# w_down by seven Strassen products, each accumulated over all pairs of feature tiles, placed behind the gate and up products

## The reference

```
x = x + rmsnorm(mix, post_mix_norm[l])
h = rmsnorm(x, pre_ffn_norm[l])
f = (jax.nn.silu(h @ ffn_w_gate[l]) * (h @ ffn_w_up[l])) @ ffn_w_down[l]
x = x + rmsnorm(f, post_ffn_norm[l])
# second layer
x32 = x.astype(jnp.float32)
y = x32 * lax.rsqrt(jnp.mean(x32 * x32, axis=-1, keepdims=True) + EPS)
z = jnp.einsum('bsd,de->bse', h, w_in)
```

## Time and profile before

| what | value |
|---|---|
| time, median of 3 runs | 2336.81 us (2334.63 to 2337.70) |
| time of the profiled execution | 2337.01 us |
| its span | 2335.1 us |
| mean granted TensorE clock | 0.973 of full speed |
| PE busy | 2153.8 us, 92% of the span, 10931 matmul instructions |
| PEld busy | 1812.1 us, 78% |
| DVE busy | 1183.2 us, 51%, 1698 instructions |
| ACT busy | 793.0 us, 34%, 1442 instructions |
| POOL busy | 906.1 us, 39%, 611 instructions |
| DMA | 125.95 MB, mean 54 GB/s |

### The profile page before, as it was taken

The page is one execution under the profiler, slowest core; times in us unless marked ns, Lnnn a source line. Parts: engine busy times, 40 slices in busy tenths (PEclk is TensorE's granted clock), DMA queues, the critical chain, the costliest instruction groups (busy, mean ns, idle before and its releaser), DMA issues. The chain is left out here.

```text
span 2335.1 us, 29185 instructions
## 1 busy us (share of the span) xinstructions
PE 2153.8 (92%) x10931; PEld 1812.1 (78%) x10931; DVE 1183.2 (51%) x1698; ACT 793.0 (34%) x1442; POOL 906.1 (39%) x611
## 2 busy tenths in 40 slices
PE   6999988688997899999999996888999999999997
PEld 5788877578775788888888875777887888888886
DVE  4443505867436735555555557678996154201132
ACT  4333225455224342222222224237775122000112
POOL 1222321332236766666666665230000332323334
PEclk9999999889999999999999997999999999999999
DMA  4121311020212111111111132210000111111131
GB/s 153 37 50 42 82 53 24 14 52 32 99 46 82 47 53 54 46 46 46 54 55 55 55 118 77 96 37 1 1 1 24 45 46 45 48 52 45 54 118 72
DMA packets 164187, 125.95 MB, mean 54 GB/s; under 512 B 25316, under 2 KB 144848, under 8 KB 163920
## 3 DMA queue, kind: packets, MB, share of 16 engines
q1 hardware_dynamic: 148576, 91.77, 13.5%
q10 hardware_dynamic: 15472, 32.31, 3.8%
HBM read 106.77 MB, written 17.30 MB: 53 GB/s over the span
## 5 line engine op out<-in xcount | busy, mean ns | idle before, releaser
L940 POOL TENSOR_SCALAR w_hi<-w_raw 128x1024 fp32r<-128x1024 f32 x113 | 130.6, 1155 | 990.2 <-issue 919.5
L1059 PE MATMUL gemm<-h_hi,w_hi 128*128 128x512 f32 x1072 | 424.3, 396 | 8.4 <-POOL h_lo L969 4.6
L1060 PE MATMUL gemm<-h_lo,w_hi 128*128 128x512 f32 x1072 | 419.6, 391 | 0.0
L1061 PE MATMUL gemm<-h_hi,w_lo 128*128 128x512 f32 x1072 | 419.5, 391 | 0.0
L943 POOL TENSOR_TENSOR w_lo<-w_raw,w_hi 128x1024 fp32r<-128x1024 f32 x113 | 283.0, 2504 | 9.4
L1059 PEld LDWEIGHTS gemm<-h_hi,w_hi 128*128 128x128 f32 x1072 | 203.0, 189 | 53.3 <-issue 8.1
L1061 PEld LDWEIGHTS gemm<-h_hi,w_lo 128*128 128x128 f32 x1072 | 202.6, 189 | 43.0
L1060 PEld LDWEIGHTS gemm<-h_lo,w_hi 128*128 128x128 f32 x1072 | 202.9, 189 | 40.6
L1873 DVE TENSOR_TENSOR acc<-acc,gemm 128x1024 f32<-128x1024 f32 x80 | 97.7, 1221 | 116.1 <-PE gemm L1080 115.9
L936 POOL TENSOR_TENSOR w_lo<-wsum,w_hi 128x512 fp32r<-128x512 f32 x100 | 136.8, 1368 | 28.4 <-ACT w_hi L1507 22.1
L1507 ACT ACTIVATE w_hi<-wsum 128x512 fp32r<-128x512 f32 x100 | 63.3, 633 | 200.3 <-POOL wsum L923 197.3
(11 more groups left out here) (413 smaller groups left out, 4404.7 us busy)
## 6 DMA issues: line engine op xcount, KB each, us to landing
w_raw<-in_w_in SPq DMA_DIRECT2D x60, 512.0 KB, 3.8
w_raw<-in_ffn_w_gate SPq DMA_DIRECT2D x22, 512.0 KB, 3.8
w_raw<-in_ffn_w_up SPq DMA_DIRECT2D x22, 512.0 KB, 4.1
w_raw<-in_ffn_w_down SPq DMA_DIRECT2D x22, 512.0 KB, 4.0
w_raw<-in_w_out SPq DMA_DIRECT2D x16, 512.0 KB, 3.7
x_spill<-x ACTq DMA_DIRECT2D x4, 2048.0 KB, 6.6
xin<-in_x SPq DMA_DIRECT2D x8, 512.0 KB, 6.4
x<-in_x ACTq DMA_DIRECT2D x1, 4096.0 KB, 15.9
```

The lines of the kernel that those rows point to most:

```text
L940: gp.tensor_scalar(hi[:], raw[key % 4][:], 1.0, 0.0, ALU.mult, ALU.add).then_inc(pool_hi, 1)
L1059: mm(o, hi[:, k, m], act[0][:, k, t], start=k == 0, stop=False)
L1060: mm(o, hi[:, k, m], act[1][:, k, t], start=False, stop=False)
L1061: last = mm(o, lo[:, k, m], act[0][:, k, t], start=False, stop=k == kt - 1)
```

## The change

w_down is no longer applied pair by pair within the gate and up loop. Now all the gate and up products come first (`f` of every pair is kept: most of it in SBUF, 16 blocks of 128x512 are written to DRAM and read back), and behind them stands a stage of seven products M4, M7, M1, M5, M3, M2, M6, each accumulated in four banks over 11 pairs: 77 items `("dm", (i, x))` of 12 matmuls. The two-by-two blocks are: of f, the feature tile of the pair (m) by the half of the tokens (t); of w_down, the same feature tile by the half of the columns. Product i reads one f block or a sum or difference of two, and one weight block or a sum or difference of two. Even products use the side banks, odd ones the gemm banks (`SIDE`). After each product its four banks are copied (ACT) or added or subtracted (DVE) into `acc`, at items `("de", (i, c))` four blocks into the next product.

For each block n the work is: DVE adds or subtracts two f blocks (`fsum`, L2196 of the kernel after; in M7, M1, M5, M2 and M6, since M4 and M3 read a single block) and two weight blocks (`wsum`, L853; in M4, M7, M1, M3 and M6); ACT rounds both to `ring_0` (L1706) and `w_hi` (L1679); DVE subtracts to get `ring_1` (L2205) and `w_lo` (L862). The ring and the weight slots each hold four blocks. At item x DVE does the sums of block x+5 and the low parts of block x+4. SP loads the one or two weight blocks of 256 KB of each item by a DMA each, and at blocks 5 and 12 of the list eight 256 KB blocks of f each from DRAM. POOL has only the gain multiplications in this stage (item `dsq`), and the last of these is on DVE. The post norm, the residual and the next norm of the first half of the tokens are within M2 and M6 (items `rows`, `res`, `nsq`, `nk`); those of the second half come after the first halves of the two q2 units.

The core of the diff:

```diff
+DOWN = (
+    ("M4", [(1, 1)], None, SUB, [(1, 0), (0, 0)], [(0, 0, None), (1, 0, None)]),
+    ("M7", [(1, 0), (1, 1)], SUB, ADD, [(1, 0), (1, 1)], [(0, 0, ADD)]),
+    ("M1", [(0, 0), (1, 1)], ADD, ADD, [(0, 0), (1, 1)], [(0, 0, ADD), (1, 1, None)]),
+    ("M5", [(0, 0), (1, 0)], ADD, None, [(1, 1)], [(0, 1, None), (0, 0, SUB)]),
+    ("M3", [(0, 0)], None, SUB, [(0, 1), (1, 1)], [(0, 1, ADD), (1, 1, ADD)]),
+    ("M2", [(0, 1), (1, 1)], ADD, None, [(0, 0)], [(1, 0, ADD), (1, 1, SUB)]),
+    ("M6", [(0, 1), (0, 0)], SUB, ADD, [(0, 0), (0, 1)], [(1, 1, ADD)]),
+)
+SIDE = (0, 2, 4, 6)
+CLOSING = (6,)
+PAIRS = tuple(range(9)) + (10, 9)
+ND = len(PAIRS)
...
-        if p + 1 < NF // 2:
-            run([("down", (p - 1, h, x)) for h in range(2) for x in range(4)])
         s += [("mul", (by["up", 2 * p], i)) for i in range(7)]
-    s.append(("load", 8))
-    run([("down", (NF // 2 - 2, h, x)) for h in range(2) for x in range(4)])
-    s.append(("load", 9))
-    run([("down", (NF // 2 - 1, h, x)) for h in range(2) for x in range(2)])
-    s.append(("rows", (1, 0)))
-    run([("down", (NF // 2 - 1, 0, x)) for x in range(2, 4)])
-    s += [("resid", (1, 0)), ("nsq", (2, 0))]
-    run([("down", (NF // 2 - 1, 1, x)) for x in range(2, 4)])
-    s.append(("rows", (1, 1)))
-    begin([("q2", 4), ("q2", 0)], [("norm", (2, 0)), ("load", 1), ("nsq", (2, 1))],
-          [("norm", (2, 1)), ("load", 2)])
+    between = {(4, 2): [("load", 8)], (4, 6): [("dsq", (0, 0))], (5, 3): [("dsq", (0, 1))], (5, 4): [("rows", (1, 0))],
+               (5, 5): [("res", 0)], (5, 6): [("res", 1)], (5, 7): [("res", 2)], (5, 8): [("res", 3)], (5, 9): [("nsq", (2, 0))], (6, 2): [("load", 9)], (6, 4): [("load", 1)],
+               (6, 6): [("dsq", (1, 0))]}
+    for i in range(7):
+        for x in range(ND):
+            s += [("dm", (i, x))] + [("de", (i - 1, x))] * (0 <= i - 1 not in CLOSING and x < 4) + between.get((i, x), [])
+            s += [("nk", x - 2)] * (i == 6 and 2 <= x <= 9)
+        if i in CLOSING:
+            s += [("de", (i, c)) for c in range(4)] + [("dsq", (1, 1)), ("dt", i)]
+    begin([("q2", 4), ("q2", 0)],
+          [],
+          [("rows", (1, 1)), ("resid", (1, 1)), ("nsq", (2, 1)), ("norm", (2, 1)), ("load", 2)])
...
# SP
+                if w in (down0 + 5, down0 + 12):
+                    part = int(w == down0 + 12)
+                    if part == 0:
+                        sp.wait_ge(f_out, 16 * len(spilled))
+                    gemm_product(sp, (last_up, 6 if part else 4))
+                    for key, n in sorted(spilled.items(), key=lambda x: x[1]):
+                        if n // 8 == part:
+                            sp.dma_start(f_at[key][:], f_dram[n]).then_inc(f_in[part], 16)
...
# PE
+            def down(i, x):
+                at_end = i in CLOSING and x >= ND - 2
+                if at_end and x == ND - 2:
+                    return
+                blocks = (ND - 2, ND - 1) if at_end else (x,)
+                for y in blocks:
+                    pe.wait_ge(w_split, job_of["dm", i, y] + 1)
+                    pe.wait_ge(N["d_low"], ND * i + y + 1)
+                for c in range(4):
...
+                        mm(o, f[0][:, hslice(c)], hi, start=y == 0, stop=False)
+                        mm(o, f[0][:, hslice(c)], lo, start=False, stop=False)
+                        last = mm(o, f[1][:, hslice(c)], hi, start=False, stop=y == ND - 1)
...
# DVE
+                elif kind == "dm" and (j[0] not in CLOSING or j[1] < ND - 2):
+                    n = ND * j[0] + j[1]
+                    block_sum(n + 5)
+                    weight_sums(it)
+                    block_low(n + 4)
+                    weight_lows(it)
...
# POOL
+                elif kind == "dsq" and j != (1, 1):
+                    t, h = j
+                    pool.wait_ge(gain_loaded, 32)
+                    for pair in range(2):
+                        pool.wait_ge(N["sq_part"], 16 + 8 * t + 4 * h + 2 * pair + 2)
+                        x = acc[:, 4 * t + 2 * pair:4 * t + 2 * pair + 2, 512 * h:512 * h + 512]
+                        step(gp.tensor_tensor(x, x, over(gbc2[:, 512 * h:512 * h + 512], 2), ALU.mult), "acc_gained")
```

## The result

The changed kernel takes 2318.4 us (median of 4 runs, 2317.6 to 2320.3) where the kernel before took 2336.5 on the same chip: a ratio of 0.9924, 95% interval 0.9907 to 0.9942. I had said 2310 with a range of 2295 to 2338. Every median here is of runs that agree with one another; one of the four runs of the kernel with the read-backs spread took 7460.6 us, which nothing on record explains, and is left out of its median. The profiled executions differ by 16.6 us (spans 2335.1 and 2318.5).

What follows compares the result with a forecast made beforehand. PE bounds the old loop, DVE the new stage from M7 on. DVE's queue of 236.7 us plus 5.4, 15.6 and 3 gives 260.7 against 287.5 before: 26.8 saved, 2310 us, range 2295 to 2338.

Steps and rivals of the forecast that it cites:

- my signs of being wrong: Down stage and loop: DVE idle in M7 while PE waits, `wsum` waiting for `w_raw`, clock clearly under 1, gate/up gaps.
- item 5 (low part of block 9): Start of the down stage: DVE, held by loads, is through at about 20.5 us, and PE isn't held up.
- items 39 to 49: Down stage, second of two stretches of eleven blocks with three DVE instructions each, plus additions: 26.7 us of DVE's queue.
- The wait behind the second 2 MB: Within items 6 to 27: DVE waits about 3.6 us for block 12's weights behind the second read-back of f.
- slower, by the loads: Rival for the down stage: w_down loads and f share SP's queue, blocks take longer, 2352 us; chance 0.06.
- The lock: Items 50 to 60: POOL's gain multiplications hold up DVE instructions with two SBUF inputs, four times 2.4, 9.6 us.
- my tail: From the last down matmul to the second norm half: additions, squares, gain, residuals and norm, 15.6 us.
- The cold clock: After the stage: PE idle for nearly 5 us, then at a lower clock for a while, costing 3 us.
- What I had at nothing: Gate and up loop without down products: keeps its length, no gaps in the products.
- The PE-bound stage at 2287: Rival: the lock costs little and reads stay hidden, so PE bounds the stage; 2287 us, half 2298; together chance 0.16.
- Hand-overs: Rival: crossings between DVE, ACT and PE expose 0.3 us on each of 71 items, 2331 us; chance 0.20.
- The clock: Rival: PE's waits in M2 to M6 lower its clock, blocks take 5.4 us, 2350 us; chance 0.08.

Runs made afterwards that it cites:

- The control without Strassen: Changed kernel's order, read-backs one by one, with eight ordinary block products (1056 matmuls, not 924) and no sums of f or weights: 2314.8 us.

## Why the prediction was right, and where its sum was off

**The order of things held.** DVE is the bound from M7 on; PE's waits are on DVE's `w_lo`; POOL's gain multiplications make single DVE instructions last 2.3 to 2.8 us; the down stage has 924 matmuls. The experiments carry this: 39.9 us added to DVE cost 32.9. One of my signs of being wrong came all the same: waits of `wsum` for `w_raw`, 11.5 us.

**Term by term**, where DVE finishes its last step of a block (us from the start of the stage, predicted and then measured): item 5 (low part of block 9) 20.5 and 26.4; items 6 to 27 69.9 and 70.6; M5's stretch 26.7 and 26.9; the next, items 39 to 49, 26.7 and 31.5; items 50 to 60 with the first residual 43.3 and 42.5; items 61 to 71 with the last `h_lo` 48.2 and 48.5; item 72 1.4 and 3.5. The sum is 236.7 against 249.8. Then 5.4 and 6.8 us to the last matmul, and 15.6 and 18.8 us to the second norm half: 257.7 against 275.4.

**The step that was mis-sized is the loads.** "They can start when the fourth-last product is done, so block 5's weights land at about 7 to 8 us" forgot that SP's queue is in order. The read-backs stand behind block 4's loads, which wait for DVE's first `w_lo`; they go out 2.0 us after the start of the stage, block 5's loads at 6.7, and `wsum` of block 5 starts at 13.35. From there DVE did the five blocks up to item 5 without a wait, in 13.0 us as my sum had it, so all of the 5.9 us (26.4 in place of 20.5) lies in that landing. PE, which I had as not held up there, waited 3.9 us in the first 16. "Items 39 to 49: 26.7" had no load at all in it, though item (4,2) in the same table of the change issues 2 MB on the other queue: 4.8 us. Spreading both gave back 9.9 of these 10.7 in the median, 8.6 in the traces. The wait behind the second 2 MB, 3.6 us in my sum, was right (3.77). I had put a price on transfers as a rival ("slower, by the loads", 2352) and not in the sum where they belonged, at a tenth of that size.

**The lock.** 9.6 us predicted for `dsq` inside items 50 to 60, at 2.4 us for each of four instructions. The three gain multiplications of two instructions each cost DVE 9.9 in all, but not all there: four lengthened instructions are inside (7.8 us), one is the last item's `w_lo` (the 2.1 us of item 72), and POOL's low part of the next weights, which my tail didn't have, hits the gain multiplications on DVE. That pair took 4.89 us where two undisturbed ones take 2.45: 2.4 of the 3.2 us by which the tail is longer.

**The cold clock** came to the size that I gave it, for a longer wait than I had: in 1437 to 1446 us PE is idle for 7.9 us, not nearly 5, and the windows of PE after it (columns as in the earlier trace rows) are

```profile
1446.00:1460.00 14.00, 14.00 (x87) 13.11 (x86) 6.01 (x8) 5.50 (x8) 0.00 (x0) 0.85 0.23 90
```

where the same work before was at 1.00. From the start of the second norm half to the end the kernel takes 873.0 us, before 869.9: 3.1 for the 3 us predicted. The same happens inside the stage, behind the 8.0 us wait: 0.67 in 1395 to 1401 us, part of it at the 1.2 GHz level. There it is free: where the transposes come one item later, the clock is at 1.00 in 1392 to 1410 us and the time is the same (2318.3).

**What I had at nothing** came out as a gain: the gate and up loop, without its down products, takes 382.7 us from 787.45 to 1170.11, where it took 389.9 before with the down products' 195.9 taken off. The 7.2 us can be placed: before, PE stood for 2.86 us, waiting for nothing that the profile shows, ahead of the sixth of its second set of gate products, 5.5 us before the first down matmul,

```profile
806.13 0.47 PE L1125 MATMUL gemm<-h_hi,w_hi 128*128 128x512 f32 x1 [2.86 <-issue]
```

which with the slower start behind it is 3.1 us. The rest are nine short gaps, each in front of the second up product behind a set of down products: 0.8 us at 836.87 (0.57 of it for POOL's `w_lo`) and eight times 0.4. The control without Strassen has none of them either, so they belong to the old place. What causes them is not tested.

**The balance**: 26.8 forecast, less 17.7 by which the stage and tail are longer, less 0.1, plus 7.2 in the loop and 0.4 ahead of it, makes 16.6, the difference of the two spans. That the number came within 8.4 us is partly luck: the unforeseen gain in the loop covers 7 of the 17.7 us by which the stage and tail were too short; without it the time would have been near 2326, inside the range but outside the forecast's own 2301 to 2322.

**The rivals.** The PE-bound stage at 2287 is not to be had by relieving DVE alone: with all weight sums gone the time is 2299 to 2300, and the waits that are left (2.2, 3.0 and 6.5 us above) lie where residuals, `acc` additions, norm steps and POOL's gain multiplications stand; which of these holds PE was not tested. Hand-overs: DVE waits 2.9 us for ACT's `ring` in all 75 instructions, so no. The clock: 0.97 over the stage and 0.92 in the last third, harmless. The loads: right in kind, wrong in size.

**What the forecast never asked** is what Strassen has to do with it. It counted 29.9 us of PE saved as the gain. The control shows that the place can give all the gain by itself (22.1 us with spread read-backs, against 18.1 for the change): the tail behind the loop, 91.6 us for 192 matmuls before, is filled with work. Of the seven products' own saving some 4 to 6 us are left once the loads are spread. That DVE's queue takes the rest fits its waits, and TensorE without a gap in the control.

## What to carry to other kernels

Before a change that saves work on one engine by adding work to another, add up the second engine's queue instruction by instruction, with the additions, residuals and loads that share it; and build the control with only the reordering, since it may hold the whole gain. When one engine's queue is the bound, look for its waits (here 11.5 us for loads), not for the longest wait in the trace: the 8.0 us of TensorE was worth nothing. Here it paid to place a group of transfers one by one between the loads that such an engine waits for, and to cut up a large one.

## What the runs showed of the hardware

- A GpSimd sum of 128x512 that runs beside VectorE takes 1.54 us in the mean (1.29 undisturbed) and in this kernel costs VectorE about as much as doing it: 33.1 us of longer instructions and 10.6 us of waits for 38.1 us of relief and some 13 us of its waits for loads. I had expected a loss or a gain, not an even trade.
- The VectorE instructions that GpSimd lengthened in the changed kernel's stage all have two SBUF inputs (2.3 to 2.8 us in place of 0.69); those with a PSUM input kept their 0.69 to 0.78 us beside GpSimd's.
- Both engines pay for meeting: two gain multiplications of VectorE took 4.89 us beside GpSimd's low part in place of 2.45, and that low part took 3.24 us where the one before it took 2.40.
